# State space mixer of a two-block network: tables in PSUM, gain in the input matrix, another order of time steps, sums in PSUM

## What is computed

```
h  = x + s5_mixer(rmsnorm(x, mix_norm[0]), ...)        # 64 groups of 16 channels, 64 complex states each
dt = exp(log_dt); lam_bar = exp(lam * dt); b_bar = ((lam_bar - 1) / lam) * b
bu = einsum(u, b_bar); state[t] = lam_bar * state[t-1] + bu[t]
y  = real(einsum(state, c)) + d_skip * u
z  = gelu(y); out = (z @ w_glu)[:, :1024] * sigmoid((z @ w_glu)[:, 1024:])
```

## Time and profile before

| | |
|---|---|
| median of 3 runs | 2554.24 us (2549.49 to 2554.86) |
| profiled execution | 2558.3 us, its span 2556.6 us |
| PE busy | 2386.2 us, 93% |
| DVE busy | 1495.4 us, 58% |
| ACT busy | 860.3 us, 34% |
| POOL busy | 221.5 us, 9% |
| mean granted TensorE clock | 0.942 |

### The profile page before, as it was taken

One profiled execution on the slowest core, in us unless ns is written; L12 is line 12 of the kernel. 1 busy time (PEld: TensorE's weight loads), 2 busy tenths in 40 slices (PEclk: granted clock), 3 DMA queues, 4 the chain that ended last, 5 costly groups with the idle time before them and its releaser, 6 DMA issues.

```text
span 2556.6 us, 30522 instructions
## 1 busy us (share of the span) xinstructions
PE 2386.2 (93%) x10966; PEld 1960.0 (77%) x10966; DVE 1495.4 (58%) x2012; ACT 860.3 (34%) x1283; POOL 221.5 (9%) x146
## 2 busy tenths in 40 slices
PE   1498999999989989999999999999998899999999
PEld 0457878888878877888886678887888688888887
DVE  8975555444766667544546747875446546754453
ACT  1112332222345443322233324553434334332221
POOL 6700220000300003000011000001000000300000
PEclk7555999999999999999999989999999999999999
DMA  2025322222211112223222221212223212222222
GB/s 102 0 41 116 105 93 99 96 93 99 99 61 59 51 42 85 97 99 99 93 96 74 74 75 50 66 58 91 98 98 126 89 50 91 94 96 99 99 95 86
DMA packets 77029, 213.19 MB, mean 83 GB/s; under 512 B 18304, under 2 KB 26752, under 8 KB 76544
## 3 DMA queue, kind: packets, MB, share of 16 engines
q1 hardware_dynamic: 57312, 199.90, 23.6%
q10 hardware_dynamic: 19616, 11.91, 2.2%
HBM read 203.26 MB, written 4.19 MB: 81 GB/s over the span
## 4 chain that ended last, share of the span: by engine, by line
PE 82%; DVE 10%; ACT 4%; issue 2%; ACTq 1%; DMA 0%; POOL 0%; DVEq 0%; POOLq 0%
PE lin L384 24%; PE lin L385 24%; PE lin L386 24%; DVE w_lo L1112 2%; ACT w_hi L758 2%; PE sc L468 1%; PE tr L456 1%; PE sc L482 1%; PE tr L554 1%; DVE t L1139 1%; DVE tmp_w L1237 1%; DVE t L1138 1%; DVE ssm_wt L1240 1%; DVE ssm_wt L1239 1%; DVE fox_pl L1397 1%
## 5 line engine op out<-in xcount | busy, mean ns | idle before, releaser
L758 ACT ACTIVATE w_hi<-w_raw 128x1024 fp32r<-128x1024 f32 x369 | 390.8, 1059 | 1075.6 <-PE lin L386 1074.7
L384 PE MATMUL lin<-x_hi,w_hi 128*128 128x512 f32 x1472 | 596.6, 405 | 3.9 <-DVE w_lo L1112 2.2
L385 PE MATMUL lin<-x_lo,w_hi 128*128 128x512 f32 x1472 | 577.0, 392 | 0.0
L386 PE MATMUL lin<-x_hi,w_lo 128*128 128x512 f32 x1472 | 576.6, 392 | 0.0
L1112 DVE TENSOR_TENSOR w_lo<-w_raw,w_hi 128x1024 fp32r<-128x1024 f32 x369 | 469.3, 1272 | 96.4 <-ACT w_hi L758 95.9
L384 PEld LDWEIGHTS lin<-x_hi,w_hi 128*128 128x128 f32 x1472 | 279.2, 190 | 71.6 <-issue 9.5
L385 PEld LDWEIGHTS lin<-x_lo,w_hi 128*128 128x128 f32 x1472 | 279.5, 190 | 65.5 <-issue 9.6
L386 PEld LDWEIGHTS lin<-x_hi,w_lo 128*128 128x128 f32 x1472 | 278.8, 189 | 59.5
L384 PE MATMUL lin<-q_hi,w_hi 128*128 128x512 f32 x704 | 274.9, 390 | 8.0 <-DVE q_lo L1117 7.2
L385 PE MATMUL lin<-q_lo,w_hi 128*128 128x512 f32 x704 | 274.6, 390 | 0.0
L386 PE MATMUL lin<-q_hi,w_lo 128*128 128x512 f32 x704 | 274.4, 390 | 0.0
(11 more groups left out here) (384 smaller groups left out, 2999.7 us busy)
## 6 DMA issues: line engine op xcount, KB each, us to landing
w_raw<-w SPq DMA_DIRECT2D x369, 512.0 KB, 3.3
ssm_mt<-ssm_kp ACTq DMA_DIRECT2D x64, 64.0 KB, 2.6
ssm_u<-x_a SPq DMA_DIRECT2D x1, 2048.0 KB, 12.4
resid<-x_b ACTq DMA_DIRECT2D x1, 2048.0 KB, 8.1
z_scratch<-ssm_y ACTq DMA_DIRECT2D x32, 64.0 KB, 2.4
z_b<-z_scratch SPq DMA_DIRECT2D x4, 512.0 KB, 3.9
out<-resid SPq DMA_DIRECT2D x8, 256.0 KB, 2.1
mem_x<-mem ACTq DMA_DIRECT2D x1, 1024.0 KB, 5.3
```

What stands on the lines that cost most here:

```text
L384: nc.tensor.matmul(out, WH[:, b, w], xh[:, k, 0:cols], start=(k == 0), stop=False)
L385: nc.tensor.matmul(out, WH[:, b, w], xl[:, k, 0:cols], start=False, stop=False)
L386: last = nc.tensor.matmul(out, WL[:, b, w], xh[:, k, 0:cols], start=False, stop=(k == KC - 1))
L758: nc.scalar.activation(WH[:, b, :], raw[:, r, :], ACT.Copy).then_inc(s_hi, 1)
```

## The change

- The operands that DVE used from SBUF in the coefficients and the input weights are now partly in PSUM: fr, fi, 1/rms, the second power tables (XTP, YTP), the temporary products (TBA, TW). ACT copies the power tables there and to XT, YT. CL has powers 0 to 7 and serves both kernels and outputs; XTP, YTP hold powers 1 to 8.
- The gain of the norm (`gain_r`, a new input of 512 KB, third in ACT's queue) is multiplied into BBr, BBi, and not into U. The skip term is multiplied with the gain and added by POOL to `ssm_kp`, behind ACT's copy; the matmul of `d_diag` goes.
- fr and fi and the wait for vecs and cols stand ahead of the powers.
- The chunks are ordered so that the 16 elements of a scan step are contiguous. The output of the glu is put back in order when it is read from PSUM.
- The loops are written out; the Toeplitz transfers are issued half by SP, half by ACT, and ACT issues those of batch b-1 behind its copy of kernels b.
- `within` writes a PSUM bank for each batch, the outputs are added there by PE, and ACT's gelu reads it. The stores of z are half SP's, half ACT's; ACT's order is gelu of quarters 0 and 1, weight splits, gelu 2, split of z 0 and 1, gelu 3, split 2 and 3.

```diff
 @block.sync
-            sp.wait_ge(s_in[5], 32)
+            sp.wait_ge(s_in[5], 48)
             ...
+            for b in range(BATCHES):
+                sp.wait_ge(s_kd, b + 1)
+                if b >= 2:
+                    sp.wait_ge(s_yk, b - 1)
+                for j in range(CH // 2):
+                    toeplitz_rows(sp, b, j)
+            for h in range(ZP):
+                sp.wait_ge(s_z, (h + 1) * BATCHES // ZP)
+                for j in range(CH // 2):
+                    z_store(sp, h, j)
+                if 1 <= h < ZP - 1:
+                    z_load(h - 1)
+            for h in range(ZP - 2, ZP):
+                z_load(h)
 @block.tensor
-                    nc.tensor.matmul(out, B0[:, at_g, :], CL[:, at_g, 0:CH, :]..., start=True, stop=False)
-                    last = nc.tensor.matmul(out[:, 0:GC], ident[0:GC, 0:GC], DK[0:GC, at_g, :], start=False, stop=True)
+                    last = nc.tensor.matmul(SCP[0:GC, g * P:(g + 1) * P], B0[:, at_g, :],
+                                            CL[:, at_g, :, :]..., start=True, stop=True)
+            def within(b):
+                pe.wait_ge(s_mt[b % 2], 16 * CH * (b // 2 + 1))
+                if b == BATCHES - 2:
+                    pe.wait_ge(s_kp, 2 * BATCHES)
+                for g in range(GB):
+                    last = nc.tensor.matmul(WB[b][:, g * NK:(g + 1) * NK], MT[:, b % 2, g, :], U[:, b * GB + g, :],
+                                            start=(g == 0), stop=False)
+                last.then_inc(s_yk, 1)
+            kernels(0)
+            pe.wait_ge(s_vr, BATCHES)
+            for b in range(1, BATCHES):
+                kernels(b)
+                within(b - 1)
+            within(BATCHES - 1)
             ...
+                    last = nc.tensor.matmul(WB[b][:, g * NK:(g + 1) * NK], CL[:, at_g, :, :]...,
+                                            S[:, at_g, :], start=False, stop=(g == GB - 1))
 @block.scalar
-            for dst, name in ((Bre, "b_re"), (Bim, "b_im")):
+            for dst, name in ((Bre, "b_re"), (Bim, "b_im"), (GR, "gain_r")):
             ...
+            act.wait_ge(s_pow, 1)
+            for first, x, y in ((0, XT, YT), (1, XTP, YTP)):
+                j = slice(first, first + CH)
+                nc.scalar.activation(x[top], LR[top, j, :], ACT.Copy).then_inc(s_xt, 1)
+                ...
+            def kernels(b):
+                act.wait_ge(s_k, b + 1)
+                if b >= 2:
+                    act.wait_ge(s_mt[b % 2], 16 * CH * (b // 2))
+                for j in range(2):
+                    nc.scalar.activation(KP[0:GC, b % 2, ...], SC[j][0:GC, :]..., ACT.Copy).then_inc(s_kp, 1)
+            def toeplitz(b):
+                act.wait_ge(s_kd, b + 1)
+                if b >= 2:
+                    act.wait_ge(s_yk, b - 1)
+                for j in range(CH // 2, CH):
+                    toeplitz_rows(act, b, j)
             kernels(0)
+            for b in range(1, BATCHES):
+                kernels(b)
+                toeplitz(b - 1)
+            toeplitz(BATCHES - 1)
             ...
+            gelus(0)
+            gelus(1)
             act.wait_ge(s_state, 2)
             for s in (-2, -1):
                 split_hi(Slab(s, 0, None, 0))
+            gelus(2)
+            z_split(0)
+            z_split(1)
+            gelus(3)
+            z_split(2)
+            z_split(3)
 @block.vector
+            dve.wait_ge(s_in[2], 32)                       # ahead of the powers
+            after(STT(out=A_["fr"], ...)); after(STT(out=A_["fi"], ...))
             ...
+            for out, f0, f1, op in ((BBr, fr, fi, ALU.subtract), (BBi, fi, fr, ALU.add)):
+                TT(TBA, Bre[:], f0, ALU.mult).then_inc(s_step, 1)
+                TT(out[:], Bim[:], f1, ALU.mult).then_inc(s_step, 1)
+                dve.wait_ge(s_step, c.up(s_step, 2))
+                after(TT(TBA, TBA, out[:], op))
+                after(TT(out[:], TBA, GR[:], ALU.mult))
-            TT(U[:], V[:], SA["rms"]..., ALU.mult).then_inc(s_u, 1)
+            TT(U[:], U[:], SA["rms"]..., ALU.mult).then_inc(s_u, 1)
             ...
+                TT(TW, chan(BBi), tab(YTP), ALU.mult).then_inc(s_step, 1)
+                if b:
+                    dve.wait_ge(s_wtt, b)
+                TT(WT[:], chan(BBr), tab(XTP), ALU.mult).then_inc(s_step, 1)
+                dve.wait_ge(s_step, c.up(s_step, 2))
+                TT(WT[:], WT[:], TW, ALU.add).then_inc(s_wt, 1)
             ...
-                t = t[:, g, :].rearrange("p g (b i) -> p g b i", i=SI)
-                return t[:, :, :, i] ...
+                return t[:, g, i * SB:(i + 1) * SB]
             ...
-            for b in range(BATCHES):
-                dve.wait_ge(s_yr, b + 1)
-                dve.wait_ge(s_y2, b + 1)
-                TT(ys, ys, SC[b % 2][:], ALU.add).then_inc(s_ysum, 1)
 @block.gpsimd
-            g_.tensor_tensor(V[:], U[:], SA["gain"]..., ALU.mult).then_inc(s_ug, 1)
             after(g_.memset(KP[0:GC, :, :, :, :], 0.0))
             ...
+            for b in range(BATCHES):
+                pool.wait_ge(s_kp, 2 * (b + 1))
+                lag0 = KP[0:GC, b % 2, :, CH - 1, :]
+                g_.tensor_tensor(lag0, lag0, DK[0:GC, b * GB:(b + 1) * GB, :], ALU.add).then_inc(s_kd, 1)
```

More of the change, by code:

```diff
@@ L283, in two_blocks @@
         MO = (SC[2], TR[2])
+        XTP, YTP = (LIN[i][:].rearrange("p (j g) -> p j g", j=CH) for i in range(2))
+        TW = SCP[:].rearrange("p (g j c) -> p g j c", g=GB, j=CH)
+        for i, n in enumerate("fr fi var rms".split()):
+            SA[n] = SC[2][:, i * G:(i + 1) * G]
+        TBA = SCP[:].rearrange("p (g c) -> p g c", c=GC)
+        IN = (SC[2], TR[2])
+        WB = (LIN[0], LIN[1], TR[0], TR[1], SC[2], TR[2], SC[0], SC[1])
         def sem(name):
@@ L437, in inflow @@
                                             start=True, stop=True)
                 last.then_inc(s_vk, 1)
-            pe.sem_inc(s_wtt, 1)
             transposes(0)
[L441 to L458, removed]
@@ L478, in _ @@
                     pe.wait_ge(s_state, b // (BATCHES // 2) + 1)
[L479 to L484, removed]
+                for g in range(GB):
+                    at_g = b * GB + g
+                    last = nc.tensor.matmul(WB[b][:, g * NK:(g + 1) * NK], CL[:, at_g, :, :].rearrange("p j c -> p (j c)"),
+                                            S[:, at_g, :], start=False, stop=(g == GB - 1))
                 last.then_inc(s_y2, 1)
-                if b == 0:
-                    within(BATCHES - 1)
             stage("glu", QH, QL, ready=chunks())
@@ new lines, in inflow_read, with kernels @@
+            def inflow_read(b):
+                act.wait_ge(s_vk, b + 1)
+                nc.scalar.activation(V[:, b * GB:(b + 1) * GB, :].rearrange("p g k -> p (g k)"), IN[b % 2][:], ACT.Copy).then_inc(s_vr, 1)
+            inflow_weights(0)
+            for b in range(1, BATCHES):
+                inflow_weights(b)
+                inflow_read(b - 1)
+            inflow_read(BATCHES - 1)
+            def kernels(b):
+                act.wait_ge(s_k, b + 1)
+                if b >= 2:
+                    act.wait_ge(s_mt[b % 2], 16 * CH * (b // 2))
@@ new lines, in gelus, with z_split @@
+            def gelus(h):
+                for b in range(h * BATCHES // ZP, (h + 1) * BATCHES // ZP):
+                    act.wait_ge(s_y2, b + 1)
+                    nc.scalar.activation(Y[:, b * GB:(b + 1) * GB, :].rearrange("p g k -> p (g k)"), WB[b][:], ACT.Gelu_apprx_tanh).then_inc(s_z, 1)
+                act.wait_ge(s_z, (h + 1) * BATCHES // ZP)
+                for j in range(CH // 2, CH):
+                    z_store(act, h, j)
+            def z_split(h):
+                act.wait_ge(s_zb[h], 16)
+                for k in range(h * KC // ZP, (h + 1) * KC // ZP):
+                    hi(QH[:, k, :], ZB[:, k, :])
@@ new lines, in _ @@
+            dve.sem_inc(s_tab, 1)
+            dve.wait_ge(s_usum, 1)
+            nc.vector.tensor_reduce(SA["var"], AUX[:].rearrange("p (g k) -> p k g", k=NK), axis=AX.X, op=ALU.add).then_inc(s_v, 1)
+            dve.wait_ge(s_rt, c.up(s_rt, 2))
+            after(STT(out=SA["root"], in0=SA["rms_a"], scalar=-0.5, in1=SA["rms"], op0=ALU.mult, op1=ALU.mult))
+            after(STT(out=SA["root"], in0=SA["var"], scalar=EPS, in1=SA["root"], op0=ALU.add, op1=ALU.mult))
+            after(STT(out=SA["rms"], in0=SA["root"], scalar=1.5, in1=SA["rms"], op0=ALU.add, op1=ALU.mult))
```

248 lines of the change are left out of this document (101 added, 147 removed).

## The result

| | before | after |
|---|---|---|
| median | 2551.86 us (2548.44 to 2554.86) | 2515.61 us (2511.20 to 2520.03) |
| profiled execution | 2558.3 us | 2511.2 us (span 2509.5) |
| mean granted clock | 0.942 | 0.961 |

The ratio is 0.9858, with its 95% interval 0.9842 to 0.9874: 36 us less. The forecast was 2534 us, with a range of 2518 to 2554.

The account below looks back on a forecast made before the run. After about 262 us comes a matmul row the diff leaves alone; only the front, a chain through DVE then PE, changes. The first glu column moves from 262.2 to 241.5, 20.5 us less: median 2534 us, range 2518 to 2554.

Parts of the forecast that it names:

- Part 1: Start of DVE's chain: cols there at 20.5, powers ready at 30.4, U ready at 47.1 against 72.1.
- Part 2: Input weights: DVE's three operations 1.22 us each beside POOL, 3.75 a batch; kernels start at 92 instead of 142.
- POOL's eight batches ... delay nothing: Input weights: POOL's eight batches run from 33 to 85 beside DVE and hold nothing up.
- Part 3: Kernels and Toeplitz: within waits for ACT's late transfers; rounds 14.4 us against 9.2, stretch 110 us, before 81.6.
- Part 4: Outputs and tail: eight output batches at 3.0 us; first glu column at 241.5, 39.5 after outputs begin; 1 us lost.
- A: Rival, Toeplitz rounds: SP and ACT take turns issuing, 1.8 to 2.5 us a round, 2547 to 2551 us; chance 0.18.
- B: Rival, input weights: operands in PSUM do not free DVE from POOL; kernels start 41 us later, 2575 us; chance 0.07.
- C: Rival: full clock in input weights, rounds and outputs, halving PE's part of each round, 2489 us; chance 0.05.
- D: Rival, Toeplitz rounds: ACT's late half does not hold PE; rounds 8 us, 45 us less, 2489 us; chance 0.04.

Follow-up runs that it names:

- experiment 1: Changed kernel, but ACT issues its four Toeplitz transfers of batch b right behind kernels b, not those of b-1: 2492.29 us, ratio 0.9763.
- experiment 2: Changed kernel, but SP issues all eight Toeplitz transfers of a batch and ACT none: 2495.65 us, ratio 0.9773.
- experiment 3: Changed kernel, but power tables and the input-weight product back in SBUF, so DVE's 24 operations have two SBUF operands: 2549.45 us, ratio 0.9990.
- experiment 5: Version of experiment 1 with the strided scan steps of the kernel before: 2492.31 us, ratio 0.9772.
- experiment 11: Version of experiment 1, plus vecs and cols early in ACT's queue and last gelus ahead of the second quarter's split: 2480.75 us, ratio 0.9714.
- experiment 7: Kernel of experiment 6, with SP issuing its four transfers only when all eight of the batch before have landed: 2520.80 us, ratio 0.9884.
- experiment 6: Changed kernel, but ACT issues transfers of batch b-1 only when its copy of kernels b has ended: 2530.61 us, ratio 0.9919.
- experiment 4: Kernel before the change, with the contiguous scan steps alone: 2551.12 us, ratio 0.9993.
- experiment 9: Version of experiment 1, with ACT's last gelus ahead of the split of the second quarter of z: 2489.67 us, ratio 0.9753.
- experiment 10: Changed kernel, with three unused 128x512 matmuls on PE between kernels b and within b-1 in five rounds: 2507.78 us, ratio 0.9821.
- experiment 12: Version of experiment 11, with three additional 128x512 matmuls on PE before within 0, 2 and 4: 2482.59 us, ratio 0.9727.

## Why the prediction missed

**Part 1, right to within the spread of one landing.** U was ready at 42.5, forecast 47.1. Of the 4.6 us, 4.1 are cols, which landed at 16.4 where I had 20.5. That is a matter of the single execution: with the same queue DVE went on at 20.2 to 20.9 in the profiled executions of experiments 1 to 3, and at 16.3 in that of experiment 5. It may be why the profiled pair differs by 41 us in the front and the medians by 36; only profiled executions have traces, so this is argued and not shown. The rest of the part stood: DVE waited there (0.95 us here, 4.6 in experiment 1), and the clearing of KP, which held one operation for 2.14 us at 7.21, delayed nothing that the wait did not cover. With the powers, the eight operations on 128x1024 and the product with rms each near its count, nothing here missed by over half a microsecond.

**Part 2, the mechanism right, one size wrong.** Each operation took 1.22 us beside POOL, as taken from the earlier trace rows; experiment 3 shows the other end. Transposes began at 46.17. From there to the first kernels I had 41 us (50.9 to 92), the middle between a clock that stays low and one that rises after the third batch. It took 33.3 (46.17 to 79.43): the clock rose already during the second inflow, and DVE's 3.66 us a batch set the pace, PE waiting 0.84 us each time. My lower end, 86, less the 4.6 of part 1, is 81.4. The middle was no forecast; the rows of before had shown the rise with these same two kinds of matmul, and I should have given it the larger weight. The upper end was off as well: eight batches of 5.45 from 50.9 end at 94.5, not at 97, and the middle of 86 and 94.5 is 90. The whole step is worth 8 us.

"POOL's eight batches ... delay nothing" was wrong in a small way. They ended at 80.8 near the forecast (85, less the 4.6), but `d_diag` and the addition stand behind them on POOL, and these release the first transfers at 85.87. I had not followed POOL to its own next step. ACT could have issued at about 84.6 in the changed kernel, at 80.3 in experiment 11.

**Part 3, the step that failed.** It is the sum for one round, 14.4 us, which laid the two copies, four issues and a landing one behind the other and took 0.54 us for each matmul of the kernels. The order of waits was right: PE idled before each within until ssm_mt landed, and undoing the order gave 23 us (experiment 1). But the rounds were 12.5 us. Term by term, in the round from 105.86 to 118.63:

- kernels 3.54 and not 4.3, 0.8 less. The 0.54 of the earlier trace rows is a matmul that alternates with one of `d_diag`; taking those out saved 0.26 a group (from a period of 0.70 in that row of matmuls to 0.44), and not the 0.16 that was counted for them.
- the wait from the end of kernels to within 5.58 and not 6.5, 0.9 less. Three things lie in it. I counted the fourth issue twice, 0.65 too much: the chain's landing begins behind the last but one, so that in experiment 7, where all is in series, copy, three issues and landing give 5.5 (1.08, 1.92, 2.42). The copy is not in series: the first issue starts beside it, 1.07 less. And SP's four go out beside ACT's, which gives 0.8 back in the landing (3.51, and 2.69 counted; 2.42 when SP is silent).

The stretch from the first kernels to the outputs was 97.8 us instead of 110. Of these 12.2, six rounds give 11.5 and the start up to the end of the first within 1.8 (its kernels ran at the upper level, 1.9 us a batch, while POOL's addition and a landing of 5.13, with both queues issuing at once, took a part of that back); the last within came 1.1 us later than counted, because PE waited for its transfers too. That terms of opposite sign hide behind a right sum shows in experiment 6: with the copy in series and both queues at once, the round is 14.9 and the time 2530.6, close to the forecast of 14.4 and 2534 by luck, since the forecast had neither the fourth issue right nor the price of the second queue. One reading of the kernel before was incomplete too: it waits for the transfers at the last batch as well, 1.43 us ahead of 219.91; no term rests on it.

**Part 4, about right, too small by 4.** Outputs to column 43.75, forecast 39.5. The outputs take 27.5 and not 24: in the earlier trace rows the row of 112 matmuls is seven batches, the first having run before it; a batch is 3.42 us. The order of ACT's splits and gelus did what was said; undoing it is worth 1 to 3 us by the traces of experiment 9, where I had called the tail as a whole a loss of 1. The scan was hidden: it ended at 145.6, PE came at 177.24, and experiments 4 and 5 give the contiguous steps no value from both sides.

**The sum.** Against the forecast: part 1 4.6, part 2 8.0, rounds 12.2, tail -4.3 give 20.5 us, the whole difference in the profiled pair. For the medians, which are 36 apart where 20 were forecast, parts 2 to 4 give 15.9, so they agree if part 1's 4.6 drops out.

**The rivals.** A was half right: SP and ACT do slow each other, but by some 1 us a round (3.51 against 2.42) and not 1.8 to 2.5, because ACT's issues start before SP's; started together it costs 2.3 a round (14.9 in experiment 6, 12.6 in 7), as A said. B is excluded by the result, and experiment 3 shows that it was the question on which all turned; there it costs 34 us, and I had priced it at 41. C came in part 2 alone. Experiment 10 shows that the clock of part 3 is not fixed either. D did not happen; experiment 1 gives its round of 8.0 us, but it is worth 23 us by the medians (27.8 from kernels to outputs in the traces) and not 45, since the rounds that it replaces take 12.5 and not 14.4 and the waits at the first and the last batch stay.

The range was too narrow on the low side: the forecast's own low end took the rise of the clock (86) and rounds of 13.2, but no row excluded an overlap of issue and copy, and the range's lower bound had no place for it.

What stays open: what exactly PE must do for the clock to rise in the rounds. The outputs stay at 0.50 without a gap, and experiment 12 gained nothing with the same fills.

## What to carry to other kernels

When an edit takes a long stall away, follow every engine to its next step: here the time went to the order of ACT's issues (23 us), to POOL's tables and to a 4.5 KB load at the end of a queue (a wait of 4.6 us). A small transfer that the first computation waits for is issued first. Two queues that issued small transfers at the same moment moved them no faster than one. Take a term of a sum from a row in which its neighbours are those that it will have, and check that the end of one term is not the start of the next counted twice.

## What was not expected of the hardware

- An issue on ACT's queue starts beside the ACTIVATE ahead of it (113.16 beside 113.09), if its own wait is met.
- A 64 KB transfer (16 partitions) lands after 2.4 us when one queue issues, and 4.4 us with another queue issuing at the same time; an issue takes 0.60 us alone and 0.87 to 1.06 then. One queue alone reaches the rate of both, about 95 GB/s (experiments 1 and 2).
- Three idle-time matmuls a round made the work behind them faster in some rounds (kernels 3.60 to 1.92 us a batch) and the kernel 8 us shorter; in the version of experiment 11 such fills gained nothing.
- The upper level of the clock can be granted while PE waits and be gone when it starts again (1.00 in 114 to 117 us, 0.50 at 118.63).
- A DVE operation that reads one operand from PSUM, with the table broadcast, and one from SBUF takes 1.22 us next to a busy POOL, and 2.4 to 2.7 with both in SBUF.
